# Hybrid stick-breaking / forgetting / memory attention layer on one core: per-head scales turned to rows once and repeated by transfers through DRAM, and K projected ahead of V

## The reference

```python
h = rmsnorm(x, norm_w[layer])
proj = h @ w_in[layer]
(sb_q, sb_k, sb_v, fx_q, fx_k, fx_v, f_logit, m_q, gate) = jnp.split(proj, offsets, axis=-1)
y = jnp.concatenate([merge_heads(sb_out), merge_heads(fx_out), merge_heads(m_out)], axis=-1)
yf = y.astype(jnp.float32).reshape(b, s, TOTAL_HEADS, HEAD_DIM)
yf = yf * lax.rsqrt(jnp.mean(yf * yf, axis=-1, keepdims=True) + EPS)
yf = yf.reshape(b, s, MIX_WIDTH) * out_norm_w[layer].astype(jnp.float32)
y = (yf * jax.nn.silu(gate.astype(jnp.float32))).astype(x.dtype)
x = x + y @ w_out[layer]
```

## Time and profile before

| | |
|---|---|
| median of 3 runs | 830.32 us (829.67 to 830.85) |
| profiled execution | 829.59 us, span of its instructions 827.8 us |
| PE busy | 803.7 us (97%) |
| PEld busy | 676.1 us (82%) |
| DVE busy | 579.9 us (70%) |
| ACT busy | 474.9 us (57%) |
| POOL busy | 253.9 us (31%) |
| mean granted clock of PE | 0.997 |
| DMA queue of the kernel | 88.17 MB, 32.2% of 16 engines |

### The profile page before, as it was taken

How to read it: one execution, slowest core, us unless ns; L and a number is a source line. 1 busy time by engine, 2 the same in 40 slices (tenths; PEclk the granted TensorE clock), 3 DMA queues, 4 the chain that set the end, 5 groups by cost and what they waited for, 6 DMA issues and landing times.

```text
span 827.8 us, 12264 instructions
## 1 busy us (share of the span) xinstructions
PE 803.7 (97%) x4244; PEld 676.1 (82%) x4244; DVE 579.9 (70%) x1207; ACT 474.9 (57%) x938; POOL 253.9 (31%) x382
## 2 busy tenths in 40 slices
PE   8999998999999999999999999999999998999996
PEld 8777786887888888888888888888887887888884
DVE  5746656666587976768797676879757677875575
ACT  5856776755756655775655567465555683532231
POOL 1134613224145433414542341454233111410000
PEclk9999999999999999999999999999999999999998
DMA  8124661111510431231043123104312198152532
GB/s 306 53 76 134 203 251 69 47 52 40 165 51 27 103 115 51 67 113 51 27 102 115 53 73 105 51 27 101 115 52 70 60 347 312 56 172 77 179 127 101
DMA packets 35533, 88.95 MB, mean 107 GB/s; under 512 B 3592, under 2 KB 11784, under 8 KB 34448
## 3 DMA queue, kind: packets, MB, share of 16 engines
q1 hardware_dynamic: 35472, 88.17, 32.2%
HBM read 57.72 MB, written 21.53 MB: 96 GB/s over the span
## 4 chain that ended last, share of the span: by engine, by line
PE 85%; DVE 5%; ACT 4%; issue 2%; POOL 2%; DMA 1%; SPq 0%; DVEq 0%; ACTq 0%; POOLq 0%
PE banks L748 14%; PE banks L750 14%; PE banks L749 14%; PE banks L789 10%; PE banks L889 8%; PE banks L909 4%; PE banks L908 4%; PE banks L876 4%; PE banks L875 4%; PE banks L952 2%; PE banks L929 2%; POOL w_parts L1313 1%; DMA hT<-wo_dram 1%; PE banks L846 1%; PE banks L841 1%
## 5 line engine op out<-in xcount | busy, mean ns | idle before, releaser
L748 PE MATMUL banks<-hT,w_parts 128*128 128x512 f32 x576 | 239.6, 416 | 3.9 <-DVE hT L1629 2.3
L750 PE MATMUL banks<-hT,w_parts 128*128 128x512 f32 x576 | 226.1, 392 | 0.0
L749 PE MATMUL banks<-hT,w_parts 128*128 128x512 f32 x576 | 225.4, 391 | 0.0
L1589 DVE TENSOR_TENSOR pT<-banks,pT 128x512 fp32r<-128x512 f32 x208 | 109.2, 563 | 93.2 <-ACT pT L1106 92.0
L1106 ACT ACTIVATE pT<-banks 128x512 fp32r<-128x512 f32 x208 | 93.4, 498 | 131.4 <-PE banks L889 131.2
L750 PEld LDWEIGHTS banks<-hT,w_parts 128*128 128x128 f32 x576 | 108.1, 188 | 24.4
L748 PEld LDWEIGHTS banks<-hT,w_parts 128*128 128x128 f32 x576 | 108.6, 189 | 19.8 <-issue 2.6
L1313 POOL TENSOR_TENSOR w_parts<-w_raw,w_parts 128x1024 fp32r<-128x1024 f32 x37 | 88.7, 2397 | 111.5 <-ACT w_parts L1009 111.5
L749 PEld LDWEIGHTS banks<-hT,w_parts 128*128 128x128 f32 x576 | 109.0, 189 | 12.5
L1552 DVE TENSOR_TENSOR_SCAN work<-work 128x639 f32<-128x639 f32 (+3 forms) x64 | 91.0, 1422 | 4.2 <-POOL work L1321 4.1
L1082 ACT ACTIVATE work<-banks 128x512 f32<-128x512 f32 (+2 forms) x96 | 47.7, 497 | 76.5 <-PE banks L876 57.7
(11 more groups left out here) (213 smaller groups left out, 1395.5 us busy)
## 6 DMA issues: line engine op xcount, KB each, us to landing
w_raw<-in_w_tiles SPq DMA_DIRECT2D x37, 512.0 KB, 3.6
hT<-wo_dram SPq DMA_DIRECT2D x16, 512.0 KB, 7.7
fx_heads<-fx_heads SPq DMA_DIRECT2D x8, 512.0 KB, 7.8
negL<-negL_dram SPq DMA_DIRECT2D x8, 512.0 KB, 7.4
yT_dram<-silu SPq DMA_DIRECT2D x8, 512.0 KB, 5.1
sb_heads<-sb_heads SPq DMA_DIRECT2D x8, 512.0 KB, 7.4
negL<-yT_dram SPq DMA_DIRECT2D x8, 512.0 KB, 4.9
work<-in_x SPq DMA_DIRECT2D x6, 512.0 KB, 6.8
```

The costliest lines, as they stand in the source:

```text
L748: pe.matmul(o, w[:, 0, k, :], hT[:, 0, k, tok], start=(k == 0), stop=False)
L749: pe.matmul(o, w[:, 0, k, :], hT[:, 1, k, tok], start=False, stop=False)
L750: mm = pe.matmul(o, w[:, 1, k, :], hT[:, 0, k, tok], start=False, stop=(k == KT - 1))
L1589: dve.tensor_tensor(pT[:, n % 3, 1, cols], banks[:, T_BANK + n % 2, cols], pT[:, n % 3, 0, cols].bitcast(F32), ALU.subtract).then_inc(t_lo, 1)
```

## The change

The scales of the pairs 0 to 8 are no longer spread on ACT and turned by N3. One small piece NT for a pair transposes head3 (128x16) once on PE, ACT copies the 16x128 result out of the bank, and SP stores it by two transfers (one a head, 8 partitions of 512 bytes) to a DRAM row of 1024 scales a head, waits for them, and loads each row into 64 partitions (two transfers of 256 KB). DVE then multiplies silu by these rows in SBUF, at ticks 14 and 15 of an mm phase, 12 and 13 of an fx phase, 11 and 12 of an sb phase. NT waits on PE for `r_ready`, at tick 9 (10 in phase 1). The last pair keeps its path. K stands ahead of V in all phases, which also moves the VT pieces: in phase 3 from ticks 6 and 8 to 10 and 11, in phase 4 from 6 and 8 to 8 and 11, in phase 8 they stay at 6 and 8.

```diff
     elif ph == 2:
-        names = [("G", 1), ("V", 3), ("K", 3), ("Q", 3)]
+        names = [("G", 1), ("K", 3), ("V", 3), ("Q", 3)]
     elif kind == "fx":
-        names = [("V", ph + 1), ("K", ph + 1), ("Q", ph + 1)]
+        names = [("K", ph + 1), ("V", ph + 1), ("Q", ph + 1)]
     else:
-        names = [("G", ph - 1), ("V", ph + 1), ("K", ph + 1), ("Q", ph + 1), ("G", ph)]
+        names = [("G", ph - 1), ("K", ph + 1), ("V", ph + 1), ("Q", ph + 1), ("G", ph)]
...
-N1_AT, SPREAD_TICK, N3_AT, GATE_AT = {1: 3, 0: 7}, 9, {1: 10, 0: 11}, (6, 8)
-SPREAD_LATER = {0: 2}
+N1_AT, NT_AT, GATE_AT = {1: 3, 0: 7}, 9, (6, 8)
+N3_AT = {"mm": (14, 15), "fx": (12, 13), "sb": (11, 12)}
...
-            out.append(Small("N3", c, ph - 1, UNITS * ph + N3_AT[c] + SPREAD_LATER.get(ph - 1, 0)))
+        out.append(Small("NT", 0, ph - 1, UNITS * ph + NT_AT + (1 if ph == 1 else 0)))
...
+SCALED_AT = {UNITS * ph + N3_AT[PHASES[ph][0]][i]: (ph - 1, c) for ph in range(1, N_PH) for i, c in enumerate((1, 0))}
...
+                if p.what == "NT":
+                    spread_rows(p.of, n)
+            def spread_rows(ph, n):
+                sp.wait_ge(small_done, n + 1)
+                for h in range(2):
+                    sp.dma_start(scale_dram[ph, h, :].rearrange("(t p) -> t p", p=P), head_rows[h:2 * NB:2, :]).then_inc(scale_out, 16)
...
+                sp.wait_ge(scale_out, 32 * (ph + 1))
+                for h in range(2):
+                    sp.dma_start(spread_of(ph)[h * HD:(h + 1) * HD, :],
+                                 scale_dram[ph, h:h + 1, :].broadcast_to((HD, S))).then_inc(scale_in, 16)
+            def store_rows(ph):
+                sp.wait_ge(scaled, 2 * ph + 2)
+                sp.dma_start(yT_dram[ph, :, :], silu[:, :]).then_inc(y_out, 16)
+                if PHASES[ph][0] == "fx":
+                    load_negL(PHASES[ph][1] + 1, 0)
...
-                if i == X0 - 4:
+                if i == X0 - 3:
                     load_y(0)
...
                 if n < 4:
                     store_part(n)
+                if n == 0:
+                    spread_rows(LAST - 1, small_of("NT", 0, LAST - 1))
...
+                elif p.what == "NT":
+                    pe.wait_ge(r_ready, p.of + 1)
+                    mm = pe.transpose(o[0:2 * NB, 0:P], head3[:, 0, :], ident[:, :])
...
+            def scale_rows(n):
+                act.wait_ge(small_ready, n + 1)
+                if SMALL[n].of:
+                    act.wait_ge(scale_out, 32 * SMALL[n].of)
+                act.activation(head_rows[:, :], banks[0:2 * NB, SMALL_BANK, 0:P], ACT.Copy).then_inc(small_done, 1)
...
+            def scaled_rows(ph, c, src):
+                dve.wait_ge(gy_done, 2 * ph + TURN[c] + 1)
...
+                g = silu[:, c * CW:(c + 1) * CW]
+                return dve.scalar_tensor_tensor(out=g, in0=src, scalar=out_g[:, t:t + 1], in1=g, op0=ALU.mult, op1=ALU.mult)
+            def scale_half_rows(ph, c):
+                dve.wait_ge(scale_in, 32 * (ph + 1))
+                scaled_rows(ph, c, spread_of(ph)[:, c * CW:(c + 1) * CW]).then_inc(scaled, 1)
...
-                for n in SMALL_AT[i - 2] if i >= X0 else []:
-                    if SMALL[n].what == "N3" and SMALL[n].of == LAST - 1:
-                        y_end_lo(0, SMALL[n].c)
+                if i in SCALED_AT:
+                    scale_half_rows(*SCALED_AT[i])
+                    if SCALED_AT[i][0] == LAST - 1:
+                        y_end_lo(0, SCALED_AT[i][1])
```

More of the change, by code:

```diff
@@ L566, in small_end @@
                     load_negL(PHASES[p.of][1], 1)
[L567 to L571, removed]
+                if p.what == "NT":
[4 more added lines that the diff above has]
+                    sp.dma_start(scale_dram[ph, h, :].rearrange("(t p) -> t p", p=P), head_rows[h:2 * NB:2, :]).then_inc(scale_out, 16)
+                if ph == 0:
+                    sp.wait_ge(f_scan, 1)
+                    sp.wait_ge(wo_out[1], 32)
+                if ph == 1:
+                    sp.wait_ge(wo_out[3], 32)
+                if ph % 2:
+                    sp.wait_ge(wo_half_out[0], 32 * halves_in(0, ph + 2))
+                elif 0 < ph < LAST - 1:
+                    sp.wait_ge(wo_half_out[1], 32 * halves_in(1, ph + 1))
+                if ph == LAST - 1:
+                    sp.wait_ge(part_out[1], 16)
+                sp.wait_ge(scale_out, 32 * (ph + 1))
[7 more added lines that the diff above has]
+                    load_negL(PHASES[ph][1] + 1, 0)
             def load_w_out(j):
@@ L595, in load_w_out_half @@
                         sp.wait_ge(sb_p, sb_no(UNITS * (half.load // UNITS)))
-                    sp.wait_ge(small_done, small_of("N3", 0, half.load // UNITS - 2) + 1)
+                    sp.wait_ge(scaled, 2 * (half.load // UNITS - 1))
                 else:
@@ L680, in _ @@
                     small_end(n)
+                if i in SCALED_AT and SCALED_AT[i][1] == 0:
+                    store_rows(SCALED_AT[i][0])
                 if i == 17:
@@ L1287, in _ @@
                         square_rows(n)
-                    if SMALL[n].what == "N3" and SMALL[n].of >= LAST - 1:
-                        y_end_hi(SMALL[n].of - LAST + 1, SMALL[n].c)
+                    if SMALL[n].what == "NT":
+                        scale_rows(n)
+                    if SMALL[n].what == "N3":
+                        y_end_hi(1, SMALL[n].c)
+                if i in SCALED_AT and SCALED_AT[i][0] == LAST - 1:
+                    y_end_hi(0, SCALED_AT[i][1])
                 if i == G_END_TICK:
@@ L1536, in finish_small @@
                         newton_start(head3[:, 0, :], head3[:, 1, :], head3[:, 2, :]).then_inc(r_begun, 1)
[L1537 removed]
+                elif p.what == "N3":
                     dve.wait_ge(small_ready, n + 1)
[L1539 to L1544 removed]
+                    scaled_rows(LAST, p.c, src).then_inc(small_done, 1)
+            def scaled_rows(ph, c, src):
+                dve.wait_ge(gy_done, 2 * ph + TURN[c] + 1)
+                kind, it = PHASES[ph]
+                t = it + {"sb": 0, "fx": NPAIR, "mm": 2 * NPAIR}[kind]
+                g = silu[:, c * CW:(c + 1) * CW]
[3 more added lines that the diff above has]
+                scaled_rows(ph, c, spread_of(ph)[:, c * CW:(c + 1) * CW]).then_inc(scaled, 1)
             def stick(u):
```

55 lines of the change are left out of this document (20 added, 35 removed).

## The result

The changed kernel takes 848.0 us (847.2 to 849.5, 4 runs) against 830.0 for the kernel before beside it: ratio 1.022, 95% interval 1.021 to 1.024. It is slower by 18.0 us where 2.5 were forecast. The profiled execution is one of 847.86 us, span 846.1.

The account below looks back on a forecast made before the run. PE, busy 803.7 of 827.8 us, was taken as the bound. Terms 0.5 - 1.2 - 1.2 + 1.6 - 0.4 + 3.2 = +2.5 on 829.59 gave 832.1, with 0.7 for the median 832.8; range 826.0 to 836.5.

Parts of the forecast that it names:

- The trade of VT pieces and projections: On PE's list: VT pieces and projections only trade places, so the move was given no cost.
- the store of silu: Phases 3, 5, 7: behind negL's 512 KB load it ends 1.2 us later; a stall of 0.3 each was taken.
- PE's gain: N3 leaves PE (7.1 us), NT joins (0.8): net 6.3 us, 0.7 a phase, if nothing waits.
- rival A: The cover holds: slack and shorter transfers hide the row path, only phase 1 costs 0.5; 824.7 us, chance 0.23.
- Phase 1: PE's NT waits 2.8 us for POOL, covering DVE waits of 1.5; with N3's 0.8 gain, about +0.5.
- Phases 3, 5, 7: Scale rows arrive in time, silu's store is late; N3's gain less a 0.3 stall, -0.4 us each.
- Phases 4 and 6: Scales' store waits behind the tile load, DVE stands 3.0 us for the rows; +0.8 us each for PE.
- the store might pass the tile load: Phases 4 and 6: a store on few rings might overtake the tile load, making the term nearer -0.2.
- Phase 9: load_y(3) queues behind the scales until 717.9, row 3 reaches DVE 3.7 late, PE resumes at 735.0: +3.2 us.
- the 1.4 of the moved split: Phase 9: the scaled half's split, with ACT's turn ahead, moves into DVE's work before the evacuation: 0.6 + 0.7 + 0.1.
- Phases 2 and 8: Phase 2: N3 and NT -0.7, V's one-pass evacuation -0.5, so -1.2; phase 8: -0.7 + 0.3, so -0.4.
- Rival C: DMA latency is worse by 3 us, deciding phases 4, 6 (+1.5 each) and 9 (+3): 838.8 us, chance 0.12.

Follow-up runs that it names:

- e15: As e9, but in phases 3, 5 and 7 SP issues the two key copies behind the scales' repeats: 822.2 us, ratio 0.992.
- e3: The changed kernel with SP issuing the two stores of scales ahead of the same tick's tile load, the repeats still behind it: 842.7 us, ratio 1.016.
- e10: The changed kernel with V ahead of K in all phases, the scales keeping their new path: 885.0 us, ratio 1.067.
- e2: The kernel before the change with K ahead of V in phases 2 to 8 and nothing else: 832.1 us, ratio 1.0018.
- e7: The changed kernel with SP storing silu ahead of VT's load of negL in phases 3, 5 and 7: 845.7 us, ratio 1.018.
- e5: The changed kernel with SP issuing the scales' stores and repeats ahead of the same tick's tile load in phases 3 to 7: 841.1 us, ratio 1.014.
- e4: The changed kernel with SP issuing the load of y row 3 ahead of the scales' stores and repeats in phase 9: 844.9 us, ratio 1.018.
- e11: e4 with, in addition, the splits of the scaled halves two ticks after the scaling, as before the change: 842.2 us, ratio 1.014.
- e9: The changed kernel with e5, e7, e11 and phase 1's NT at tick 11 together (825.8), and V ahead of K in phases 3, 5, 7: 845.8 us.
- e12: As e9, but with V ahead of K in all phases: 847.0 us, ratio 1.020.
- e13: As e9, but with ACT issuing the scales' stores and repeats in phases 3 to 7: 839.3 us, ratio 1.011.

## Why the prediction was wrong

The direction was right, the size by far not. Two steps failed above all. The trade of VT pieces and projections was put at nothing and, with the store of silu that came late by it, cost 8.2 of the 15.8 us that the forecast missed. And every wait was priced at its length, which left out some 5 us of half clock. Against the forecast's steps:

**PE's gain** was right: N3 away and NT in are steps of -0.44, -0.44 and +0.12, 0.76 a phase where 0.7 was forecast. In e15 it comes out, and rival A with its 824.7 was near the kernel that the new path can be, with other places in SP's list (and with phase 1's wait mended, which A kept at +0.5). Its condition, that the cover holds, is what failed.

**Phase 1** (+0.5, measured +1.64): the wait of PE for POOL was forecast as 2.8 and is 2.79, and the covered waits of 1.5 went. What failed is that the sum priced a wait at its length. In e3 and e10 the same wait came without half clock, and the phase then costs +0.1.

**Half clock** is the missing term. By phase 1 the pair of steps is 4.0 with a stretch of 3.4 us at half clock and 2.5 without, 1.5 for the stretch. Phase 6 differs from phase 4 by 1.6, and phase 9 has some 1.9 (below): 5 of the 15.8 that the forecast missed. The other large parts are 8.2 in phases 3, 5 and 7, 2.4 in phases 4 and 6 and 0.7 in phase 9.

**Phases 3, 5, 7** (-0.4, measured +1.9 and 0.7 more in the fx phase behind two of them): "VT pieces and projections only trade places" was the step that failed, with 8.2 us the largest miss. Three things came of the trade. K now ends where V did, and its evacuation takes ACT and then two passes of DVE where V's took one: 0.67 of PE's time, with or without the new path (e2). Q's two evacuations come late for PE, 0.42 and 0.51. Neither is there with the order alone (e2); the first goes with V first and the second stays (e15), so that the second belongs to the path and the first to both together. That VT and the scaling meet in DVE's list at ticks 11 and 12, where PE, relieved of N3, is sooner, is argued from the rows; no run took it apart. And the store of silu behind negL was seen, with its 4.5 to 5 us of ACT's wait (5.38), but given 0.3 where PE paid 1.0 to 1.1, and 0.7 again at the next tick 1 (e7).

**Phases 4 and 6** (+0.8; measured 2.0 and 3.6 without the 0.7 of the gate): the mechanism was right, place by place. The store landed 3.3 after its issue (3.1 forecast), the repeats took 4.7 where 3.4 were taken; the 1.3 is a term mis-sized, and passes straight to PE. Half clock is the other 1.6 of phase 6. That the store might pass the tile load, as weighed there, did not come about: 0.4 behind a tile load it took 3.3, with nothing in flight 2.5 (343.43 to 345.94 in e5), so it paid 0.8 for its place where 0.7 was forecast. With the stores ahead it was the repeats' place behind the tile load that counted (e3, e5).

**Phase 9** (+3.2, measured +5.8): load_y(3) was issued at 730.47, 0.4 behind the forecast's 717.9 and the 12.1 of shift; it took 5.4 (4.8 forecast), PE resumed 3.9 later than before, counted from the start of the phase, in place of 3.2, and the rest, 1.9, is half clock. Behind the row stood DVE's own list (e4, e11), with the 1.4 of the moved split that the forecast had counted.

**Phases 2 and 8** came within 0.3, phase 2 with luck in it: there the key copies were ahead of the scales in the changed kernel too, the repeats went out 5.8 us after the first store, and DVE waited 2.16 for the repeats, a wait that the forecast did not have and that PE did not feel. Rival C had the right sign for the DMA and the wrong size; it knew nothing of the clock and the gates either.

## What to carry to other kernels

- A round trip through DRAM in an issuing queue's list costs its place more than its bytes: 4 KB behind a waiting tile load, or beside a megabyte of copies, took 8 us and more until it had landed, and 2.5 where nothing else was in flight. Before taking work off the bound engine for it, write down what else is in flight at that tick, and put the round trip first.
- Where the bound engine has a clock that falls when it waits, one wait of 2 to 3 us can cost some 1.6 more than its length; in the profiled kernels 13 of 19 such waits did have half clock behind them. Stalls of different cause also hide each other: mended singly they gave 16 to 19, together 22, more than the 18 that the change had lost.
- A trade of two pieces is not free if they are evacuated in different ways; compare tick by tick, not by sums of busy time.

## What the runs showed of the hardware

**The clock after a wait is a matter of the execution.** The wait of 2.8 for POOL in phase 1 stands in eight of the profiled kernels; behind it the granted clock was at half in six and full in two (e3, e10). Waits of 2.47 (changed kernel) had no such stretch and of 2.40 (e4), at the same instruction, had one. Each of e9's three waits of 6.0 came with 6.8 us at half clock, which began 2 to 3 us before the wait ended (at 287.9 for the one until 290.15). And the wait of some 1.7 for the output weights in phase 9 stands in all 17 profiled kernels, the one before among them; it had 3.4 us at half clock behind it in five (e2, e5, e9, e11, e12).

**Small transfers.** Two stores of 4 KB took 1.4 us to issue where the forecast had 0.8, by rows of large transfers. Even so they had landed 2.5 after the first issue where nothing else was in flight (343.43 to 345.94 in e5), almost the 2.4 of the forecast; 3.3 with a tile load issued 0.4 ahead of them (348.41 to 351.74); and in e9, with the two key copies ahead, the issuing alone took 4.3 and the landing 7.3 to 8.4. Counted from its own issue, 0.72 after the first, the second store landed in 1.8 in e5. The forecast cited a fixed cost of 2.0 from the Trainium skill (DMA: Bandwidth & Descriptors, "Anatomy of one DMA"), which the page gives for transfers that GpSimd issues; these of SP come near it.

**DVE and POOL stop each other.** In e13's rows above, POOL's mask of 128x128, 0.29 us at the median, lasts 2.27 and ends 0.1 behind DVE's scan beside it (282.13 to 284.50); then POOL's split and DVE's product start together, and the product ends 3.37 later in place of 1.3, 1.07 after the split. The Trainium skill (SBUF — State Buffer, "SBUF: two separate sides") has the port pair that the two share as an exclusive lock: a DVE instruction with two inputs in SBUF and a GpSimd instruction that reads SBUF can't hold it together, and whichever starts first has it for its whole length. The trace agrees. A DVE that is 2 us late thus also changes whom it meets.
